# Token tiles handed one by one across four post-norm stage ends, with the post-norm's scale vectors brought by DMA

## The chip, the core and the metric

The kernel runs on one core of a Trainium2 chip. The metric is the device time of one execution in microseconds (us): 3312.12 us, the median of 3 runs (3311.99 to 3313.26). Everything is float32.

## The reference, cut to what matters

The input is 256 tokens of 2048 features, so two *token tiles* of 128 tokens. Two layers run one behind the other, and then a third block of another kind. A layer is

```python
for layer in range(2):
    h = rmsnorm(x, pre_mix_g[layer])
    mix = even_mixer(h, ...) if layer == 0 else rglru_mixer(h, ...)   # ends in ... @ w_out
    x = x + rmsnorm(mix, post_mix_g[layer])                           # stage end
    f = sq_relu_mlp(rmsnorm(x, pre_mlp_g[layer]), mlp_w1[layer], mlp_w2[layer])
    x = x + rmsnorm(f, post_mlp_g[layer])                             # stage end

def rmsnorm(x, g):
    y = x * lax.rsqrt(jnp.mean(x * x, axis=-1, keepdims=True) + EPS)
    return y * g
```

So there are four *stage ends with a post-norm*: the output of a stage (2048 features a token) is normed over all its features, scaled by a vector g of 2048 numbers, and added to the residual stream x. The new x is normed again, which is the input of the next stage's first product. End 1 follows the attention's output product, end 2 the first MLP, end 3 the recurrent mixer's output product, end 4 the second MLP. The third block ends with a final norm and its own scale vector.

## The kernel before, in words

**Products.** A weight matrix is read in *units*: two blocks of 128 rows by 512 columns, 512 KB. SyncE issues the DMA of each unit into a ring of 8 slots (`raw`). ScalarE rounds a unit to `hi` (`conv`, line 597), VectorE writes `lo = raw - hi` (line 1071); both have a ring of 4. TensorE then does three matmuls of 512 columns for each block and token tile: x_hi hi, x_lo hi, x_hi lo (`unit`, lines 1736 to 1738). A unit is thus 12 matmuls, 6 a token tile. The activations stand as the stationary operand, features on the partitions, in `xt_h`/`xt_l` and `ht_h`/`ht_l`.

**Chunks.** A *chunk* is 512 output columns, normally 8 units, summed in the PSUM pair `pair[0]`, one bank a token tile. Every engine runs the same program `model`, chunk after chunk, and each engine does its part strictly in the order in which it is written; semaphores tie the engines together. In a chunk TensorE takes the first two and the last two units token tile by token tile and the others for both, so that a chunk's first token tile can be read out while the second is still being summed. ScalarE and VectorE convert units three ahead of the chunk that they read out (`AHEAD`). The four chunks of a stage's last product go to `acc` (VectorE, `evac`: copied for "set", added for "add"), and ScalarE squares what was written (line 651) with the sums per token.

**An MLP** has four groups; each group is four "relu2" chunks and four "add" chunks. Layer 0 runs group 0 and then a hardware loop of three turns; layer 1 runs group 0, a loop of two turns, and group 3 with steps for the third block among it. GpSimd sets `acc` to zero ahead of each MLP, so that all groups can add.

**A stage end** is the first chunk of the next stage, which has a `lead` of kind "post". TensorE first spreads the scale vector: four `gain` matmuls (line 1868, two instructions each) put 512 columns of g on all partitions in the two banks `misc_ps`. VectorE waits until both token tiles of the last chunk are read out and squared, sums the squares, ScalarE takes the root (line 743), VectorE the reciprocal (`norm_factor`). Then for each 512 columns n (`residual`): acc times factor times g for two token tiles (line 1277, two instructions), x += acc for both at once (line 1281). TensorE transposes that part of x (`turn_part`, line 1894, eight transposes of 128 by 128) into `turn_ps` or `pair[1]`, ScalarE writes its `hi` with the next norm's scale (`part`, line 758, four instructions of 256 elements) and then squares x (line 770), VectorE writes the `lo` (`lo_part`, line 1298, four of 256). Parts 0 and 1 are turned ahead of the first weight matmul, part 2 behind units 0 and 1, part 3 behind units 2 and 3. Of the stage's units three are converted before the stage end begins.

**The final norm** gets its vector in the same way: a matmul behind each of the last four chunks (`spread_final_gain`, line 2159).

Of the kernel before, what the change touches and what calls it, by code (L numbers as in the profile page):

```python
# [34 lines left out]
P = 128  # L35
SEQ = 256
M = SEQ // P
D = 2048
# [20 lines left out]
G_POST_MIX, G_POST_MLP, G_FINAL, G_ROWS = 0, 8, 16, 20  # L59
# [35 lines left out]
    "squared": "scalar: sums of squares of a chunk are written, tmp is free",  # L95
# [3 lines left out]
    "gain_ready": "tensor: a chunk of a gain is spread over the partitions",  # L99
    "x_ready": "vector: a chunk of the residual stream is up to date",  # L100
    "acc_zero": "gpsimd: acc is zero for an MLP's sums",
    "gained": "vector: a chunk of x times the final gain is in acc",
# [88 lines left out]
N_LOADS, N_PARAM_LOADS = 15, 12  # L191
# [5 lines left out]
Lead = namedtuple("Lead", "kind gain_row gain_col parts x_hi x_lo")  # L197
# [35 lines left out]
def build(nc, i, out):  # L233
# [15 lines left out]
    with ExitStack() as ctx:  # L249
# [18 lines left out]
        grows = at("grows", 170, [CH])  # L268
# [104 lines left out]
        class Program:  # L373
# [26 lines left out]

            HALF = {"psum_free_act": "half_free_act", "psum_free_dve": "half_free_dve"}
# [6 lines left out]
        class Sync(Program):  # L408
            def setup(self):
# [21 lines left out]
                for dst, src in (  # L431
                    (grows[0:8], i["post_mix_g"].rearrange("l (c n) -> (l c) n", n=CH)),
                    (grows[8:16], i["post_mlp_g"].rearrange("l (c n) -> (l c) n", n=CH)),
                    (grows[16:20], i["final_g_2"].rearrange("(c n) -> c n", n=CH)),
# [22 lines left out]
            def chunk(self, kind, w, units=8, width=CH, lead=None, slot=None, prep=None, **_):  # L457
                src, t0, col0 = w
                if lead and lead.kind == "post":
                    self.T.add("x_ready", 4)  # L460
# [108 lines left out]
        class Scalar(Program):  # L569
# [112 lines left out]
            def chunk(self, kind, w, units=8, width=CH, prev=None, lead=None, to=None, dst=None, n=0, ss=True,  # L682
                      more=False, final=False, gate=None, lru=None, constant=False, slot=None, slot1=None, prep=None, bank=0,
                      **_):
                T, ps = self.T, pair[bank]
                T.add("pe", units)
                if lead:
                    self.lead(lead)
                    self.evac(kind, ps, 0, dst, width)
                    self.conv()  # L690
                else:
                    at = self.turn_slot(prev, units)
                    for j in range(units):
# [3 lines left out]
                        if prep is not None:  # L697
                            self.prepare(prep, j)
                        if slot is not None:
# [3 lines left out]
                        if j == 1 and self.unsquared is not None:  # L703
# [14 lines left out]
                        if j == 6 and lru is not None:  # L718
                            self.lru_root(lru)
                self.evac(kind, ps, 1, dst, width)  # L720
                if kind in self.TURNED:
# [6 lines left out]

            def lead(self, lead):

                kind = lead.kind
                if kind == "post":
                    self.root(D)
# [1793 lines left out]
```

## Time and profile before

| | |
|---|---|
| median of 3 runs | 3312.12 us |
| the profiled execution | 3304.36 us |
| its span in the trace | 3302.6 us |
| mean granted clock of TensorE | 0.986 |
| busy: TensorE, weight load, VectorE, ScalarE, GpSimd | 3213.3, 2638.0, 1892.6, 1594.0, 255.4 us |
| DMA | 595.37 MB, mean 180 GB/s |

The trace is one profiled execution. Busy time is the time in which an engine has an instruction under way; matmuls overlap (one of 512 columns lasts 0.39 us in the trace, though the next starts sooner), so TensorE's distance from start to start says more than its busy time. The granted clock is the share of full speed that TensorE was given. The chain of waits is followed back from the last instruction to what released it, and so names what the end depended on.

### The profile page before, as it was taken

How to read it: one execution, taken by the hardware profiler on the slowest of the kernel's cores; microseconds unless marked ns; L12 is line 12 of the kernel's file. 1: busy time of each engine (PE TensorE's matmuls, PEld its weight loads, DVE VectorE, ACT ScalarE, POOL GpSimd, SP SyncE). 2: the span in 40 equal slices, each digit the busy share in tenths (PEclk: the TensorE clock that was granted, in tenths of full speed). 3: DMA queues.
4: the chain of work that ended last, by engine and by line, in shares of the span. 5: the costliest groups of instructions: out<-in, count | busy, mean ns of one | idle time of the engine just before them, and what ended most of it. 6: DMA issues, size and time to landing. Idle time of an engine off the chain costs nothing.

```text
span 3302.6 us, 39931 instructions
## 1 busy us (share of the span) xinstructions
PE 3213.3 (97%) x15159; PEld 2638.0 (80%) x15159; DVE 1892.6 (57%) x2142; ACT 1594.0 (48%) x2197; POOL 255.4 (8%) x331
## 2 busy tenths in 40 slices
PE   8999999999999999999999999999989999999998
PEld 6777788888888787778888888878778888888886
DVE  4667654555555667555554555558876545455445
ACT  5655544444444568554444445543354543444443
POOL 0000000000000020010830005610000000000000
PEclk9999999999999999989999999989999999999999
DMA  6544556556565455555656557756545665665663
GB/s 225 147 147 141 153 184 196 187 186 191 191 186 188 146 176 164 181 153 189 193 183 196 187 186 229 237 179 194 160 131 169 187 189 191 191 191 191 192 191 115
DMA packets 321365, 595.37 MB, mean 180 GB/s; under 512 B 32740, under 2 KB 39828, under 8 KB 320936
## 3 DMA queue, kind: packets, MB, share of 16 engines
q1 hardware_dynamic: 321192, 592.98, 57.5%
q8 instruction: 119, 1.95, 0.2%
q14 instruction: 54, 0.44, 0.0%
HBM read 581.89 MB, written 11.01 MB: 180 GB/s over the span
## 4 chain that ended last, share of the span: by engine, by line
PE 90%; DVE 6%; ACT 3%; issue 1%; SPq 0%; DMA 0%; ACTq 0%; DVEq 0%
PE pair L1736 28%; PE pair L1738 28%; PE pair L1737 28%; DVE lo L1071 2%; PE turn_ps L1767 1%; ACT hi L597 1%; PE pair L2055 1%; PE pair L1949 0%; PE misc_ps L1868 0%; PE pair L2056 0%; DVE conv_o L1176 0%; PE turn_ps L1894 0%; PE pair L1894 0%; PE misc_ps L1964 0%; DVE lru_h L1352 0%
## 5 line engine op out<-in xcount | busy, mean ns | idle before, releaser
L1071 DVE TENSOR_TENSOR lo<-raw,hi 128x1024 fp32r<-128x1024 f32 x1084 | 1341.4, 1241 | 1261.8 <-ACT hi L597 1251.2
L597 ACT ACTIVATE hi<-raw 128x1024 fp32r<-128x1024 f32 x1084 | 1144.1, 1059 | 1399.2 <-PE pair L1738 1377.0
L1736 PE MATMUL pair<-hi,xt_h 128*128 128x512 f32 (+1 forms) x2784 | 1100.7, 395 | 19.2 <-DVE lo L1071 7.1
L1738 PE MATMUL pair<-lo,xt_h 128*128 128x512 f32 (+1 forms) x2784 | 1086.2, 390 | 0.0
L1737 PE MATMUL pair<-hi,xt_l 128*128 128x512 f32 (+1 forms) x2784 | 1085.1, 390 | 0.0
L1736 PEld LDWEIGHTS pair<-hi,xt_h 128*128 128x128 f32 x2784 | 526.2, 189 | 142.0 <-issue 15.7
L1738 PEld LDWEIGHTS pair<-lo,xt_h 128*128 128x128 f32 x2784 | 525.5, 189 | 110.7
L1737 PEld LDWEIGHTS pair<-hi,xt_l 128*128 128x128 f32 x2784 | 526.5, 189 | 104.1
L1736 PE MATMUL pair<-hi,ht_h 128*128 128x512 f32 x1504 | 587.6, 391 | 4.9 <-DVE ht_l L1185 3.6
L1738 PE MATMUL pair<-lo,ht_h 128*128 128x512 f32 x1504 | 585.3, 389 | 0.0
L1737 PE MATMUL pair<-hi,ht_l 128*128 128x512 f32 x1504 | 585.2, 389 | 0.0
L1736 PEld LDWEIGHTS pair<-hi,ht_h 128*128 128x128 f32 x1504 | 282.3, 188 | 66.7 <-DVE ht_l L1185 4.0
L1738 PEld LDWEIGHTS pair<-lo,ht_h 128*128 128x128 f32 x1504 | 282.3, 188 | 58.8
L1737 PEld LDWEIGHTS pair<-hi,ht_l 128*128 128x128 f32 x1504 | 282.4, 188 | 57.8
L624 ACT ACTIVATE stg<-pair,stat 128x512 f32<-128x512 f32 x126 | 86.7, 688 | 114.1 <-PE pair L1738 112.9
L2292 POOL MEMSET acc<- 128x4096 f32 x3 | 10.6, 3521 | 920.1 <-DVE xres L1281 547.2
L1111 DVE TENSOR_TENSOR acc<-pair,acc 128x512 f32<-128x512 f32 x96 | 66.0, 687 | 24.1 <-PE pair L1738 24.1
L2165 POOL TENSOR_TENSOR lru_h<-ht_h,ht_l 128x1024 f32<-128x1024 f32 x4 | 9.6, 2402 | 865.9 <-ACT gate_i L801 865.9
L1767 PE MATMUL turn_ps<-ident,stg 128*128 128x128 f32 x508 | 65.9, 272 | 0.0
L1767 PEld LDWEIGHTS turn_ps<-ident,stg 128*128 128x128 f32 x508 | 58.9, 140 | 6.8
L651 ACT ACTIVATE tmp<-acc 128x512 f32<-128x512 f32 x80 | 49.3, 617 | 19.1 <-DVE acc L1111 17.2
L1161 DVE TENSOR_TENSOR ht_l<-turn_ps,ht_h 128x1024 fp32r<-128x1024 f32 x43 | 52.4, 1219 | 4.2 <-ACT ht_h L672 4.2
(269 smaller groups left out, 1669.1 us busy)
## 6 DMA issues: line engine op xcount, KB each, us to landing
raw<-in_mlp_w SPq DMA_DIRECT2D x512, 512.0 KB, 4.1
raw<-in_w_gate SPq DMA_DIRECT2D x88, 512.0 KB, 4.2
raw<-in_w_up SPq DMA_DIRECT2D x88, 512.0 KB, 4.2
raw<-in_w_down SPq DMA_DIRECT2D x88, 512.0 KB, 4.1
raw<-in_even_w_in SPq DMA_DIRECT2D x68, 512.0 KB, 3.7
raw<-in_odd_w_in SPq DMA_DIRECT2D x64, 512.0 KB, 3.9
raw<-in_w_in SPq DMA_DIRECT2D x64, 512.0 KB, 3.9
raw<-in_even_w_out SPq DMA_DIRECT2D x32, 512.0 KB, 3.6
```

Of the source, the lines that this page charges most:

```text
L597: nc.scalar.activation(hi[:, r], raw[:, slot], ACT.Copy).then_inc(sems["hi_ready"], 1)
L624: a = nc.scalar.activation(to, ps[:, m, 0:width], func, scale=st(RS + m))
L651: a = nc.scalar.activation(tmp[:, m], src[:, m, n * CH:(n + 1) * CH], ACT.Square, accum_out=st(sums + 4 * m + n))
L1071: nc.vector.tensor_tensor(lo[:, r], raw[:, slot], hi[:, r].bitcast(F32), ALU.subtract).then_inc(sems["lo_ready"], 1)
L1111: a = nc.vector.tensor_tensor(dst[:, m], ps[:, m], dst[:, m], ALU.add)
L1161: a = nc.vector.tensor_tensor(to[1], turn_ps[:], to[0].bitcast(F32), ALU.subtract)
L1736: nc.tensor.matmul(to, xh[:, t0 + k, tok], h[:, k], start=s, stop=False)
L1737: nc.tensor.matmul(to, xl[:, t0 + k, tok], h[:, k], start=False, stop=False)
L1738: mm = nc.tensor.matmul(to, xh[:, t0 + k, tok], l[:, k], start=False, stop=e)
L1767: a = nc.tensor.transpose(turn_ps[:, k, m * P:(m + 1) * P], stg[:, m, k * P:(k + 1) * P], ident[:])
L2055: nc.tensor.matmul(to, b_w[:, j, 2 + ri], u2[:, g, 0:HALF], start=True, stop=False)
L2292: nc.gpsimd.memset(acc[:], 0.0).then_inc(sems["acc_zero"], 1)
```

## The change

- **Tiles.** At the four ends the work on x is cut in eight tiles of 512 features by 128 tokens, in the order `TILES` = (part, token tile) (0,0) (1,0) (0,1) (1,1) (2,0) (2,1) (3,0) (3,1).
- **Tail.** The last chunk of each of these stages (`tail`) takes its last *four* units token tile by token tile (before: two; in the chunk of 4 units at end 1 all four). TensorE turns tile 0 ahead of the last unit's second token tile, and tile 1 behind the chunk. ScalarE and VectorE don't convert ahead across the end: the first three units of the next stage are converted inside `post_lead`. ScalarE does a root of a constant at the end of the tail.
- **Lead.** Each token tile has its own squares, root and reciprocal. `residual` is one instruction a tile. A tile has 4 transposes, 4 ScalarE and 4 VectorE instructions of 128 elements. TensorE takes the first four units for token tile 0 and then for token tile 1, with the turns of tiles 2 to 7 in between.
- **Scale vectors.** ScalarE issues one DMA per 512 numbers, from DRAM to all 128 partitions (256 KB written), into one buffer `gain`; VectorE multiplies `acc` by it in place one chunk later (`apply_gain`), the last chunk's in the lead (`tile_gain`). A load waits until the one before is used. The final norm's vector comes in the same way. All matmuls that spread vectors go, and three DMAs of the setup.
- **Around it.** The first group of each MLP writes `acc` ("set"), GpSimd's zeroing goes; squares are taken only in the group that ends a stage; layer 0's loop has two turns and its last group stands by itself. In the tail of end 4 ScalarE's step `prepare(.., 6)` moves up to unit 4, ahead of the load of the scale vector.

```diff
@@ Scalar.chunk
-                    for j in range(units):
+                    for j in range(units - AHEAD if tail else units):
...
+                        if j == (4 if units == 8 else 0 if tail else 1) and stage is not None:
+                            name, l = STAGES[stage]
+                            self.load_gain(4 * stage + n, i[name][l, n * CH:(n + 1) * CH])
+                        if j == 3 and final:
+                            self.load_gain(16 + n, i["final_g_2"][n * CH:(n + 1) * CH])
...
+                if tail:
+                    nc.scalar.activation(unused, eps_col, ACT.Sqrt)
+                    return
+            def load_gain(self, q, src):
+                if q:
+                    self.eng.wait_ge(sems["gain_used"], q)
+                nc.scalar.dma_start(gain[:], src.partition_broadcast(P)).then_inc(sems["gain_loaded"], 16)
+            def post_lead(self, lead): 
+                self.out_square(0)
+                self.tile_root(0)
+                self.convs(2)
+                self.tile_hi(lead, 0, 0)
+                self.conv()
+                self.tile_hi(lead, 1, 0)
+                self.out_square(1)
+                self.tile_root(1)
+                self.conv()
+                self.tile_hi(lead, 0, 1)
+                self.tile_hi(lead, 1, 1)
+                for p, m in TILES[0:4]:
+                    self.x_square(p, m)
+                self.conv()
+                self.tile_hi(lead, 2, 0)
+                self.tile_hi(lead, 2, 1)
+                self.conv()
+                self.tile_hi(lead, 3, 0)
+                self.tile_hi(lead, 3, 1)
+                self.conv()
+                self.x_square(2, 0)
+                self.x_square(2, 1)
+                self.conv()
+                self.x_square(3, 0)
+                self.x_square(3, 1)
+                self.convs(2)
+                self.root(D)
@@ Vector
+                        if j == (0 if units == 4 else 3) and stage is not None and n:
+                            self.apply_gain(n - 1)
+            def post_lead(self, lead): 
+                self.sum_squares(0)
+                self.tile_gain(0)
+                self.tile_factor(0)
+                self.residual(0, 0)
+                self.residual(1, 0)
+                self.conv()
+                self.tile_lo(lead, 0, 0)
+                self.conv()
+                self.evac(*self.unread)
+                self.tile_lo(lead, 1, 0)
+                self.sum_squares(1)
+                self.conv()
+                self.tile_factor(1)
+                self.residual(0, 1)
+                self.conv()
+                self.residual(1, 1)
+                self.tile_lo(lead, 0, 1)
+                self.tile_lo(lead, 1, 1)
+                self.residual(2, 0)
+                self.residual(2, 1)
+                self.conv()
+                self.tile_lo(lead, 2, 0)
+                self.tile_lo(lead, 2, 1)
+                self.tile_gain(1)
+                self.residual(3, 0)
+                self.conv()
+                self.residual(3, 1)
+                self.tile_lo(lead, 3, 0)
+                self.tile_lo(lead, 3, 1)
+                self.convs(4)
+                self.norm_factor(SSX, RS, "rs_ready")
-                for m in range(M):
-                    ins = nc.vector.scalar_tensor_tensor(acc[:, m, cols], acc[:, m, cols], st(RPOST + m),
-                                                         misc_ps[:, n % 2], ALU.mult, ALU.mult)
-                ins = nc.vector.tensor_tensor(xres[:, :, cols], xres[:, :, cols], acc[:, :, cols], ALU.add)
+                nc.vector.scalar_tensor_tensor(xres[:, m, cols], acc[:, m, cols], st(RPOST + m), xres[:, m, cols],
+                                               ALU.mult, ALU.add).then_inc(sems["x_ready"], 1)
@@ Tensor.chunk
+                head = 4 if post or units == 4 and tail else 2
+                end = 4 if tail else 2
+                            if post:
+                                self.tile_wait(lead, j, 1 if whole else m)
+                                if (m, j) in ((0, 3), (1, 0), (1, 2), (1, 3)):
+                                    self.turn_tile(2 + ((0, 3), (1, 0), (1, 2), (1, 3)).index((m, j)))
+                            if tail and (m, j) == (1, units - 1):
+                                self.turn_tile(0)
...
+                            if post and whole:
+                                self.turn_tile(2 + j)
...
+                if tail:
+                    self.turn_tile(1)
-            def spread_final_gain(self, n):
```

## Rows read from the trace of the kernel before

**Rows 1.** The page's chain that ended last, by engine.
```profile
PE 90%; DVE 6%; ACT 3%; issue 1%; SPq 0%; DMA 0%; ACTq 0%; DVEq 0%
```

**Rows 2.** TensorE's timeline, last group: start us, us, engine, line, operation, out<-in [idle before <-releaser].
```profile
3235.98 0.39 PE L1738 MATMUL pair<-lo,ht_h 128*128 128x512 f32 x1
...
3236.66 0.39 PE L1738 MATMUL pair<-lo,ht_h 128*128 128x512 f32 x1
...
3238.03 0.50 PE L1736 MATMUL pair<-hi,ht_h 128*128 128x512 f32 x1
```

**Rows 3.** Groups by line: count | busy us, mean ns of one | idle before.
```profile
L1071 DVE TENSOR_TENSOR lo<-raw,hi 128x1024 fp32r<-128x1024 f32 x1084 | 1341.4, 1241 | 1261.8 <-ACT hi L597 1251.2
...
L597 ACT ACTIVATE hi<-raw 128x1024 fp32r<-128x1024 f32 x1084 | 1144.1, 1059 | 1399.2 <-PE pair L1738 1377.0 <-PE pair L2144 11.8 <-PE misc_ps L1917 5.7
...
L880 ACT ACTIVATE o_diff<-misc_ps 128x128 f32<-128x128 f32 x16 | 4.3, 269 | 0.0
...
L1435 DVE SCALAR_TENSOR_TENSOR probs<-scores,stat,probs 128x128 f32<-128x128 f32 x8 | 2.8, 352 | 0.3
```

**Rows 4.** TensorE's timeline, end 1.
```profile
359.96 0.39 PE L1738 MATMUL pair<-lo,xt_h 128*128 128x512 f32 x1
...
366.85 1.97 PE L1894 MATMUL turn_ps<-ident,xres 128*128 128x128 f32 x8 [4.60 <-DVE xres L1281]
...
374.65 0.80 PE L1736 MATMUL pair<-hi,xt_h 128*128 128x512 f32 x1
...
379.06 0.40 PE L1737 MATMUL pair<-hi,xt_l 128*128 128x512 f32 x1
...
382.26 1.03 PE L1894 MATMUL turn_ps<-ident,xres 128*128 128x128 f32 x8
383.05 0.48 PE L1736 MATMUL pair<-hi,xt_h 128*128 128x512 f32 x1
```

**Rows 5.** Timelines: the lead chunk's second read-out at end 1; end 4.
```profile
400.60 0.69 ACT L624 ACTIVATE stg<-pair,stat 128x512 f32<-128x512 f32 x1 [0.24 <-PE pair L1738]
...
2160.19 0.39 PE L1738 MATMUL pair<-lo,ht_h 128*128 128x512 f32 x1
...
2202.39 0.69 ACT L624 ACTIVATE stg<-pair,stat 128x512 f32<-128x512 f32 x1 [0.24 <-PE pair L1738]
```

**Rows 6.** Table loads of ScalarE ahead of line 743's root, groups by line.
```profile
L743 ACT ACT_TABLE_LOAD x5 | 6.4, 1283 | 0.1
```

**Rows 7.** Windows, end 1: stretch, busy by engine, then granted TensorE clock, DMA share, GB/s.
```profile
366.00:372.00 6.00, 5.15 (x16) 3.32 (x17) 5.61 (x10) 2.79 (x8) 0.00 (x0) 0.50 0.00 0
```

**Rows 8.** VectorE's and ScalarE's timelines, end 1.
```profile
361.32 0.68 DVE L1111 TENSOR_TENSOR acc<-pair,acc 128x512 f32<-128x512 f32 x1
362.04 0.63 ACT L651 ACTIVATE tmp<-acc 128x512 f32<-128x512 f32 x1 [1.89 <-DVE acc L1111]
...
363.40 0.16 DVE L1260 TENSOR_REDUCE stat<-stat 128x2 f32<-128x8 f32 x1 [1.40 <-ACT tmp L651]
363.60 0.29 ACT L743 ACTIVATE stat<-stat 128x2 f32<-128x2 f32 x1 [0.23 <-DVE stat L1260]
...
364.13 1.41 DVE L1277 SCALAR_TENSOR_TENSOR acc<-acc,stat,misc_ps 128x512 f32<-128x512 f32 x2
...
368.86 1.57 ACT L758 ACTIVATE xt_h<-turn_ps,col 128x256 fp32r<-128x256 f32 x4 [4.96 <-PE turn_ps L1894]
369.73 1.66 DVE L1298 SCALAR_TENSOR_TENSOR xt_l<-turn_ps,col,xt_h 128x256 fp32r<-128x256 f32 x4 [0.36 <-ACT xt_h L758]
```

**Rows 9.** DMA issues: out<-in, queue, count, KB each, median us to landing.
```profile
b_raw<-in_b_re SPq DMA_DIRECT2D x1, 256.0 KB, 4.1
b_raw<-in_b_im SPq DMA_DIRECT2D x1, 256.0 KB, 6.1
```

**Rows 10.** TensorE's timeline behind two other gaps of the kernel.
```profile
1350.13 0.50 PE L1736 MATMUL pair<-hi,ht_h 128*128 128x512 f32 x1 [3.60 <-DVE ht_l L1185]
...
2331.93 0.79 PE L2067 MATMUL misc_ps<-u,c_w 128*128 128x128 f32 x2 [3.13 <-DVE h_im L1584]
```

More of the change, by code:

```diff
@@ L94 @@
     "split_done": "vector: their lo part too, the turned PSUM is free",
-    "squared": "scalar: sums of squares of a chunk are written, tmp is free",
+    "squared": "scalar: sums of squares of a chunk, or of a token tile of it, are written, tmp is free",
     "tot_ready": "vector: the tokens' sums of squares are added up",
@@ L98 @@
     "rs_ready": "vector: its reciprocal, the stage's rms factors",
[L99 to L102, printed above, removed]
+    "gain_loaded": "a chunk of a gain is on all partitions (16 a chunk)",
+    "gain_used": "vector: it is multiplied in",
+    "x_ready": "vector: a chunk of the residual stream (of a token tile, in a lead with a norm) is up to date",
     "out_ready_dve": "vector: the first half of the features of a token tile is normed",
@@ L698, in chunk @@
                             self.prepare(prep, j)
+                            if tail and j == 4:
+                                self.prepare(prep, 6)
                         if slot is not None:
@@ L1188, in chunk @@
             def chunk(self, kind, w, units=8, width=CH, prev=None, lead=None, to=None, dst=None, n=0, ss=True,
-                      more=False, final=False, gate=None, lru=None, constant=False, slot=None, slot1=None, bank=0, **_):
+                      more=False, final=False, gate=None, lru=None, constant=False, slot=None, slot1=None, bank=0,
+                      stage=None, tail=False, **_):
                 T, ps = self.T, pair[bank]
@@ L1199, in chunk @@
                     at = self.turn_slot(prev, units)
-                    for j in range(units):
+                    for j in range(units - AHEAD if tail else units):
                         if j == units - 1:
@@ L1781, in chunk @@
                     self.eng.wait_ge(sems["k0_copied"], 8)
-                if lead:
+                post = lead is not None and lead.kind == "post"
+                if lead and not post:
                     self.lead_first(lead)
                 at = self.turn_slot(prev, units)
-                for j in range(0, units, 2):
-                    first, last = j == 0, j == units - 2
-                    for half in range(2):
-                        if j + half == at:
-                            self.turn(prev)
-                        if last and half == 0 and prev and kind in ("add", "set"):
-                            self.eng.wait_ge(sems["split_done"], T.at("split_done"))
-                        self.lead_wait(lead, j + half)
-                        self.part_wait(ready, j + half, 0)
-                        self.unit(x, ps, self.tile(x_tiles, width, j + half), first and half == 0, last and half == 1,
-                                  width, (0,) if first or last else (0, 1))
-                        if not (first or last):
-                            self.prepare(prep, j + half)
+                head = 4 if post or units == 4 and tail else 2
@@ L1798, in chunk @@
                             if slot is not None:
[L1799 removed]
+                                self.mix_at(slot + j)
                             if slot1 is not None:
[L1801 to L1815 removed]
@@ L2365, in ht_part, with mlp_group @@
             return ht_h[:, 4 * j:4 * j + 4], ht_l[:, 4 * j:4 * j + 4]
[L2367 removed]
+        def mlp_group(e, w1, w2, g, lead=None, params=False, prep=False, stage=None):
             prev = None
@@ L2375, in mlp_group @@
             for n in range(NCH):
-                e.chunk("add", (w2, g * KT, n * CH), x=HT, dst=acc_cols(n), n=n, prev=prev if n == 0 else None,
-                        more=n < NCH - 1, prep=4 + n if prep else None)
+                e.chunk("set" if lead else "add", (w2, g * KT, n * CH), x=HT, dst=acc_cols(n), n=n,
+                        prev=prev if n == 0 else None, ss=stage is not None, more=n < NCH - 1, stage=stage,
+                        tail=stage is not None and n == NCH - 1, prep=4 + n if prep else None)
                 if params and n == 1:
@@ L2399, in swiglu_group @@
             for n in range(NCH):
-                e.chunk("add", (w_down2, g * KT, n * CH), x=HT, dst=acc_cols(n), n=n, units=2 * hidden, ss=False,
+                e.chunk("set" if lead else "add", (w_down2, g * KT, n * CH), x=HT, dst=acc_cols(n), n=n, units=2 * hidden, ss=False,
                         prev=prev if n == 0 else None, more=n < NCH - 1, final=last)
```

301 lines of the change are left out of this document (181 added, 120 removed).

## The prediction

> **What bounds the kernel now.** The page's chain first: TensorE carries 90% of what the end depended on, VectorE 6%, ScalarE 3% [rows 1]. A stream of weight matmuls at full clock starts one every 0.227 us (three in 0.68 us) [rows 2], so 2.72 us a unit, 21.76 us a chunk. ScalarE needs 1.06 us and VectorE 1.24 us to convert a unit [rows 3], under half of that. So only what makes TensorE stop or run slower counts, and TensorE's timeline shows where: at the stage ends. At end 1 the last weight matmul starts at 359.96, its successor would be due at 360.19, the first of the next chunk starts at 374.65 [rows 4], and the chunk is over at 400.43 (its second read-out starts at 400.60, 0.17 behind) [rows 5]. That is 40.24 us for 21.76 us of matmuls: **18.5 us lost**. End 4, by the same three readings, loses 2202.22 - 2160.42 - 21.76 = 20.0 us [rows 5]; ends 2 and 3, by the rows of the same pattern (of which the first and the last of four stand), 18.1 and 19.4. **Sum 76.0 us.** Ends 3 and 4 hold a table load of 1.28 us that ends 1 and 2 don't [rows 6].
>
> In a loss stand: a chain over read-out, squares, root, two factors and the residual until the first transpose at 366.85, 4.60 us after TensorE had nothing left [rows 4]; then transposes at half speed, eight in 1.97 us against about 0.8 us at full speed at 382.26 [rows 4], since the granted clock is 0.50, the lower level of 1.2 GHz [rows 7]; then ten weight matmuls in 4.41 us (374.65 to 379.06), 2.1 us more than they need [rows 4].
>
> **The change at one end, step by step.** I walk the three in-order queues with these prices. Token tile of a unit on TensorE 6 x 0.227 = 1.36 us; four transposes 0.45 (half of 382.26 to 383.05, and the slower start behind them) [rows 4]. Convert: 1.06 then 1.23, the next start 0.97 and 1.15 later [rows 3]. Read-out 0.68; square of a token tile 0.73 with its sum (362.04, and the reduce starts at 363.40 after two); reduce 0.16; root 0.29; one residual instruction 0.70 (two of its shape in 1.41) [rows 8]. The 128-element instructions don't stand in a trace with these operands. Upper bound: the 256-element ones, four in 1.57 and 1.66, so 0.39 and 0.41 each [rows 8]. Lower: half, 0.20. The step from 512 elements (0.70) to 256 (0.41) takes off 0.15 per 128 on VectorE, so 0.27; ScalarE 0.28, for which 128 elements out of PSUM at 0.269 speak [rows 3] (VectorE's nearest lasts 0.352, of which its successor waits less). I take 0.27 and 0.28: a tile is about 1.1 us on each.
>
> A rule of the Trainium skill weighs against small tiles here. In "VectorE: DVE Perf Modes", section "The TRN2 errata", it says that every instruction pays a fixed latency, and to use 512 elements or more. By its figures (120 cycles and the elements at 0.96 GHz) an instruction of 128 is an estimate of 0.26 us, so the sum is the same by either; halving the instruction doesn't halve its price, and that is in it.
>
> Zero is the end of the tail's token tile 0. Read-out to 0.86, square to 1.63, reduce, root to 2.16; VectorE's scale multiply meanwhile; reciprocal, residual of tile 0 at 2.57 to 3.31, of tile 1 to 3.97. TensorE needs the first at 4.08, after three units of token tile 1: **no wait for tile 0**, and none for tile 1. The tail ends at 6.34, with its two turns in it. Units 0 and 1 of the next stage need their conversion: ScalarE 2.12 to 4.14, VectorE at 3.90 and, behind tile 0's lo, at 6.35. TensorE starts at 6.34, unit 1 at 7.70.
> - Unit 2 stands in VectorE's queue behind read-out 1, tile 1's lo and the second reduce, and is ready at 10.49. TensorE waited from 9.06: **1.46**. Unit 3: **0.20**.
> - Token tile 1 of units 0 to 3 runs with turns 3 to 5 in between until 20.7. Unit 4 needs tile (2,1)'s first half, which is behind four squares and a conversion on ScalarE and a conversion and tile 4 on VectorE: ready 21.9. **1.25**.
> - Units 4 and 5, turns 6 and 7, until 28.28. Unit 6 is queued behind tile 7: hi to 29.53, convert 30.50, lo of the unit 31.77. **3.52**, the longest. Unit 7 stands behind two squares: **0.84**.
> - The next chunk waits for the read-out, which waits for the norm factor: **0.63**.
>
> Waits 7.9 us, eight turns 3.6 us: **11.5 us lost per end, 46.0 for four.** With 0.41 and 0.39 a small instruction the same walk gives 14.7 us, with 0.20 it gives 9.9.
>
> **The scale vectors.** The loads of an end's last vector go out just before it is wanted (1.77 in the walk, and TensorE has 0.77 of slack at tile 0). At ends 2 and 3 ScalarE issues it behind the tail's unit 7, near -4; at end 4 only behind the moved `prepare` copies, near -1.4; at end 1 behind the multiply of vector 2, near -1.6. 256 KB loads land 4.1 and 6.1 us after issue [rows 9]; a broadcast of one row stands nowhere, so these are my bounds. At 4.1 nothing waits at ends 1 to 3, at 6.1 ends 1 and 4 wait 2 us. I take 0.5 each: **1.0**. If the vectors are late, what is queued behind the multiply is VectorE's reciprocal and both residuals, and TensorE at turn 0. The other 15 loads have half a chunk or more, and sit in ScalarE's idle time; a load waits for the multiply before it, behind it ScalarE's conversions, which have three units of lead.
>
> **The clock.** TensorE comes into the end at full clock and no longer stands still for 4.6 us. Of its new gaps only the 3.52 (and a turn before it) is near those after which rows show the lower level: a gap of 3.60 left matmuls at full speed (0.50 us), one of 3.13 was followed by slow ones (0.79) [rows 10]. Even chances; a fall costs up to the 2.1 us of above, less the 0.84 and part of the 0.63 that it covers. I take 0.8 an end: **3.2**. The Trainium skill, "TensorE: Matmul & The Clock Gate", section "Why this matters for your kernels", warns that an idle gap between bursts of matmuls throws the clock back. Taken to hold at every end it would make this term 6.4, so 3 us more.
>
> **The rest.** Of the final norm's four matmuls three stand between chunks: 3236.66 to 3238.03 plus a slow second matmul, less 0.23, is 1.24 us each [rows 2]: **-3.7**; the fourth stands beside the last read-out. Layer 0's loop loses a turn: between nothing and 0.6, I take **-0.5**. The root of a constant takes the 1.28 us table load out of the chain of ends 3 and 4 (it lies in ScalarE's wait for the tail; without that cover it would cost its 1.28); this is already in the walk. VectorE's scale multiplies move into chunks where it is idle for half the time, GpSimd's zeroing and 48 chunk squares were on no path: nothing. Costs nothing as well: a "set" instead of an "add".
>
> **Sum.** 76.0 - 46.0 - 1.0 - 3.2 + 3.7 + 0.5 = **30 us less**. The profiled execution took 3304.36 us (span 3302.6), so 3274 by it. It ran 7.8 us under the median of the runs; I take the same difference off the median: 3312.1 - 30 = **3282 us**.
>
> **The rivals.**
> - *Small instructions cost like large ones.* VectorE and ScalarE lengthen the waits to 14.7 an end, the ends cost 12.7 more: 3295. For it: the fixed part is most of an instruction already. Against: 0.269 for 128 elements out of PSUM. 15%.
> - *The gaps shrink.* Small instructions at 0.20 and no fall of the clock: 9.9 an end, 9.6 less: 3272. 10%.
> - *The vectors come late at all four ends.* The landing decides: from about 6 us on ends 1 and 4 wait, from 7 us all four. At 10 us each end waits some 5 more and the clock falls: about 25 us, 3307, no change that counts. For it: a DRAM row read 128 times on a queue that nothing used before. 6%.
> - *Slower: the clock stays low through the lead.* Its place is the stretch from the wait for unit 2 to that for unit 6. If each of the gaps of 1.46, 1.25 and 3.52 us drops the clock, products take 2.72 us a token tile and turns twice as long; all of a lead at half speed adds 21.8 + 3.6 less the 7.9 of waits that it covers, 17.5 an end, 70 in all: 3350. It decides from 8.3 us an end, nearly half of the lead at half speed. For it: a 3.13 us gap did it [rows 10]. Against: the 3.60 us one didn't, and two of the three here are under half of that. 7%.
> - *The waits don't move as written*, for instance a conversion stays behind and the end is as long as before, less the gain matmuls: 3306. 4%.
>
> **How the numbers follow.** My forecast has 58% with a range of its own of 3275 to 3292. The cases with 15% and 10% are faster too. Time from no change can be told at about 0.2%, 6.6 us, so faster is under 3305.5: 58 + 15 + 10 and half of the late vectors and unmoved waits, 0.88. Within: 0.05. Slower: 0.07. The range leaves out the slow clock and half of the two cases near no change above, and half of the shrunk gaps below: 3270 to 3303.
>
> **What would show it.** In the trace after: tile 0's transposes start within 0.5 us of a matmul, with no idle before; TensorE's gaps at an end are four or five, the longest near 3.5 us just ahead of unit 6, released by VectorE's conversion; from the tail's last product to the lead's second read-out about 32.5 us where it was 40.4; a tile's four small instructions take 1.1 to 1.2 us; the granted clock is 1.00 in each end but for at most one dip; line 2159's matmuls are gone. It is wrong if turn 0 waits for a scale vector, if the clock is 0.5 for more than a unit or two, or if the lead is as long as before.

## The result

| | us, median (runs) | ratio to the kernel before, 95% interval |
|---|---|---|
| kernel before | 3312.47 (4) | 1 |
| changed kernel | 3280.05 (4; 3277.36 to 3282.88) | 0.9902 [0.9885, 0.9919] |
| changed kernel, repeated later (after_again) | 3282.89 (4), before 3308.99 (15) | 0.9915 [0.9900, 0.9930] |

The change is worth 26 to 32 us; 3282 (3270 to 3303) was predicted. That the first median lies within 2 us of the forecast is partly luck: the four executions of the changed kernel spread over 5.5 us, and the repeat gives 6 us less of a gain than the first comparison. The profiled execution of the changed kernel took 3277.36 us, its span is 3274.8, which is 27.8 under the span of before. The page's chain that ended last, by engine, where [rows 1] stood:
```profile
PE 88%; DVE 7%; ACT 4%; issue 1%; DMA 0%; SPq 0%; ACTq 0%
```
and the windows of the four ends (stretch, busy by engine, granted clock, DMA share, GB/s), where [rows 7] showed 0.50:
```profile
358.00:400.00 42.00, 34.90 (x162) 26.73 (x161) 29.88 (x61) 28.59 (x69) 0.00 (x0) 1.00 0.44 138
1082.00:1124.00 42.00, 35.03 (x165) 27.51 (x164) 30.24 (x61) 29.09 (x69) 0.00 (x0) 1.00 0.42 133
1405.00:1447.00 42.00, 36.17 (x165) 28.59 (x164) 30.47 (x62) 29.28 (x69) 0.00 (x0) 0.96 0.40 113
2138.00:2180.00 42.00, 36.03 (x163) 28.14 (x162) 30.64 (x61) 29.12 (x69) 8.26 (x10) 0.96 0.49 153
```
TensorE is busy for 35 to 36 of 42 us, and the clock dips briefly at ends 3 and 4 alone.

TensorE's gaps at end 2 of the changed kernel, from its timeline (start us, us, engine, line, operation, out<-in [idle before <-releaser]):
```profile
1086.21 0.39 PE L1901 MATMUL pair<-lo,ht_h 128*128 128x512 f32 x1
1086.44 0.60 PE L2018 MATMUL turn_ps<-ident,xres 128*128 128x128 f32 x4
1086.80 0.48 PE L1899 MATMUL pair<-hi,ht_h 128*128 128x512 f32 x1
...
1092.76 0.47 PE L1899 MATMUL pair<-hi,xt_h 128*128 128x512 f32 x1 [1.12 <-DVE lo L1164]
...
1104.60 0.50 PE L1899 MATMUL pair<-hi,xt_h 128*128 128x512 f32 x1 [1.42 <-DVE xt_l L1420]
...
1114.58 0.47 PE L1899 MATMUL pair<-hi,xt_h 128*128 128x512 f32 x1 [3.31 <-DVE lo L1164]
...
1116.95 0.47 PE L1899 MATMUL pair<-hi,xt_h 128*128 128x512 f32 x1 [0.74 <-DVE lo L1164]
...
1121.69 0.50 PE L1899 MATMUL pair<-hi,xt_h 128*128 128x512 f32 x1 [0.38 <-ACT stg L631]
```
These answer to [rows 4]: where TensorE stood for 4.60 us and then turned at half speed, the first transposes follow a matmul after 0.23 us, and what is left is five short stops, ahead of unit 2, unit 4, unit 6, unit 7 and the next chunk. The three longer stops (1.1 to 1.2, 1.4 and 3.3 us) stand at all four ends, the two short ones (0.74 and 0.38) only at ends 1 and 2, where the clock did not fall. Here are ScalarE and VectorE ahead of the longest stop:
```profile
1111.09 1.14 ACT L831 ACTIVATE xt_h<-pair,col 128x128 fp32r<-128x128 f32 x4 [2.07 <-PE pair L2018]
1112.11 1.07 ACT L604 ACTIVATE hi<-raw 128x1024 fp32r<-128x1024 f32 x1
1113.05 0.64 ACT L813 ACTIVATE tmp<-xres 128x512 f32<-128x512 f32 x1
```
```profile
1111.75 1.13 DVE L1420 SCALAR_TENSOR_TENSOR xt_l<-pair,col,xt_h 128x128 fp32r<-128x128 f32 x4 [2.08 <-ACT xt_h L831]
1113.21 1.23 DVE L1164 TENSOR_TENSOR lo<-raw,hi 128x1024 fp32r<-128x1024 f32 x1 [0.33 <-ACT hi L604]
```
Unit 6's conversion (line 604, then 1164) is queued behind the last token tile, and TensorE starts 0.14 us after VectorE is through. A tile's four small instructions take 1.11 to 1.16 us on either engine.

At end 1 the last vector is late (VectorE's timeline):
```profile
358.31 0.69 DVE L1202 TENSOR_TENSOR acc<-pair,acc 128x512 f32<-128x512 f32 x1 [1.19 <-PE pair L1901]
...
360.75 0.69 DVE L1407 TENSOR_TENSOR acc<-acc,gain 128x512 f32<-128x512 f32 x1 [0.80 <-DMA gain<-in_post_mix_g]
361.36 0.15 DVE L1390 RECIPROCAL stat<-stat 128x1 f32<-128x1 f32 x1
```
ScalarE issued that load at 357.15, and VectorE had it 3.6 us later, after an idle time of 0.80 us. Turn 0 starts at 362.36, that is 0.17 us after its place in the stream of matmuls, and in the repeat TensorE idles 0.44 us ahead of it. By the DMA view, the loads of one row to all partitions took:
```profile
gain<-in_post_mix_g ACTq DMA_DIRECT2D x8, 256.0 KB, 4.2
gain<-in_post_mlp_g ACTq DMA_DIRECT2D x8, 256.0 KB, 4.2
gain<-in_final_g ACTq DMA_DIRECT2D x4, 256.0 KB, 3.2
```

**Where the 27.8 us are.** The loss of an end after is counted as before, to the lead's second read-out: the time from the read-out of the tail's first token tile, less 27.2 us of matmuls (5.44 of the tail, 21.76 of the chunk).

| part | before | after | difference |
|---|---|---|---|
| four ends | 18.5 + 18.1 + 19.4 + 20.0 = 76.0 | 13.5 + 12.7 + 12.7 + 13.1 = 52.0 | -24.0 |
| final norm, from end 4 to VectorE's last read-out | 1087.47 | 1083.64 | -3.8 |
| gaps on TensorE in layer 0's loop | 0.74 + 0.55 | none | -1.3 |
| a fall of the clock in the stage ahead of end 3 | 0.60, 0.54 in two 4 us windows | 0.75, 0.82 | -1.7 |
| two falls of the clock in the attention stage that before's trace lacks | | | +3.4 |
| rest | | | -0.4 |

The two rows on falls of the clock, and part of the loop's, lie between executions and not between kernels. The two falls in the attention stage stand in every trace of this study but before's, that of before_loop_two (the old kernel there) among them; and the repeat of the changed kernel has a gap of 0.89 us at the loop, and a span of 3280.9. No run separates the tiles from the way in which the vectors come; the 24 us belong to both together.

### The profile page after: what moved, and what is told of

The parts are those of the page before. It is cut to its first block, busy times and chain, and to the rows that moved or that the text cites. A ratio compares the mean times of both kernels' runs of the same rounds, so it can differ in the third digit from the quotient of the medians.

```text
span 3274.8 us, 39528 instructions
## 1 busy us (share of the span) xinstructions
PE 3179.9 (97%) x15119; PEld 2621.4 (80%) x15119; DVE 1903.4 (58%) x2218; ACT 1579.9 (48%) x2173; POOL 247.5 (8%) x328
## 4 chain that ended last, share of the span: by engine, by line
PE 88%; DVE 7%; ACT 4%; issue 1%; DMA 0%; SPq 0%; ACTq 0%
PE pair L1899 28%; PE pair L1901 27%; PE pair L1900 27%; DVE lo L1164 2%; ACT hi L604 1%; PE turn_ps L1930 1%; PE pair L2228 1%; PE pair L2122 1%; PE pair L2229 0%; DVE xt_l L1420 0%; DVE conv_o L1267 0%; ACT tmp L813 0%; PE misc_ps L2137 0%; DVE lru_h L1516 0%; ACT xt_h L831 0%
## 5 line engine op out<-in xcount | busy, mean ns | idle before, releaser
L1202 DVE TENSOR_TENSOR acc<-pair,acc 128x512 f32<-128x512 f32 x72 | 49.5, 687 | 26.0 <-PE pair L1901 26.0
L679 ACT ACTIVATE ht_h<-turn_ps 128x1024 fp32r<-128x1024 f32 x43 | 43.5, 1012 | 0.1
L1179 DVE TENSOR_TENSOR stg<-stg 128x1024 f32<-128x1024 f32 x32 | 39.1, 1222 | 0.0
```

Of the source, the lines that this page charges most:

```text
L679: nc.scalar.activation(to[0], turn_ps[:], ACT.Copy).then_inc(sems["split_hi"], 1)
L1179: nc.vector.tensor_tensor(stg[:], stg[:], stg[:], ALU.mult).then_inc(sems["staged"], 1)
L1202: a = nc.vector.tensor_tensor(dst[:, m], ps[:, m], dst[:, m], ALU.add)
```

## The experiments

All but the last are the changed kernel with one edit (order_loads has two). "End" is the time from the read-out of the tail's first token tile to the lead's second read-out, in each run's trace.

| run | us (runs) | ratio to before | ends 1 to 4, us |
|---|---|---|---|
| after_again | 3282.89 (4) | 0.9915 [0.9900, 0.9930] | 41.1, 39.9, 39.9, 41.8 |
| conv_first | 3279.30 (4) | 0.9910 [0.9895, 0.9926] | 39.4, 38.2, 40.2, 38.6 |
| squares | 3273.99 (4) | 0.9890 [0.9871, 0.9909] | 40.1, 37.6, 38.5, 38.0 |
| order | 3261.09 (5) | 0.9852 [0.9838, 0.9865] | 32.4, 32.3, **42.4**, 33.1 |
| loads_only | 3281.27 (4) | 0.9912 [0.9896, 0.9929] | 41.0, 39.9, 39.9, 40.2 |
| order_loads | **3249.03** (5) | **0.9817** [0.9803, 0.9830] | 32.3, 32.4, 32.4, 33.1 |
| tail_two | 3289.55 (4) | 0.9937 [0.9921, 0.9952] | + 2.7 at 2 to 4: 44.1, 42.5, 42.5 |
| no_root | 3281.87 (4) | 0.9915 [0.9900, 0.9931] | 41.2, 40.0, 40.9, 41.8 |
| before_loop_two | 3310.34 (10) | 1.0003 [0.9994, 1.0012] | |

(The kernel before took 3307.8 to 3309.0 beside these. In tail_two the first token tile's read-out comes 2.7 us later at three ends, which is added.)

**conv_first.** The conversions go ahead of the last tiles:
```
 Scalar:  tile_hi(lead, 2, 1)            Vector:  residual(3, 1)
-conv(); tile_hi 3,0; tile_hi 3,1; conv() -tile_lo 3,0; tile_lo 3,1; convs(4)
-x_square 2,0; 2,1; conv()
+convs(3); tile_hi 3,0; tile_hi 3,1      +conv(); tile_lo 3,0; conv(); tile_lo 3,1; convs(2)
+x_square 2,0; 2,1
```


> The changed kernel, with the conversions of units 6 and 7 of the lead moved ahead of tile (3, 1)'s two copies on ScalarE, and on VectorE ahead of tile (3, 0)'s and tile (3, 1)'s lo parts. Theory (my forecast's): the 3.3 us gap ahead of unit 6 and the 0.75 us behind it are the order of the conversions alone. Both then go, but the norm factor of the next chunk hangs on the same chain of squares and residuals; a walk of the three queues with the trace's durations gives a loss per end of 11.5 us where it gives 13.45 now, with a new wait of about 3.9 us ahead of units 8 and 9's second read or the read-out: 4 x 1.9 = 8 us faster, about 3272. Rival A: the gap is all there is, and nothing waits later: 4 x 4.1 = 16 us faster, about 3264. Rival B: the tiles become late instead, ahead of units 6 and 7, by as much as the conversions went ahead: within 2 us of 3280. The clock at the ends: if it falls by the idle time of 3.3 us, it falls in neither unit 6's place at any end.

Both gaps went, and 3.26 us stood ahead of the next chunk instead (5.2 at end 3). TensorE's timeline at end 2:
```profile
1122.93 0.50 PE L1901 MATMUL pair<-hi,xt_h 128*128 128x512 f32 x1 [3.26 <-ACT stg L631]
...
1124.22 0.52 PE L1903 MATMUL pair<-lo,xt_h 128*128 128x512 f32 x1
1124.54 0.63 PE L1901 MATMUL pair<-hi,xt_h 128*128 128x512 f32 x1
```
The end is 1.7 us shorter there (1.9 expected), and by the next chunk's first read-out nothing is left: 60.30 us from the same start, 60.35 in the changed kernel. At ends 1 and 3 that read-out even comes 0.8 to 1.7 us later than in the changed kernel and its repeat. The matmuls of 0.63 us behind the wait are the clock: it fell in or around the new wait at all four ends, and no stop stands right behind it that could take the fall in. So the gap that was filled came back as a wait in the next chunk, and what remained went to the clock. At end 3 there is a third part: ScalarE idles 1.50 and 0.42 us ahead of two conversions there, for weights that SyncE issued late (see order). Rival A has fallen, and so has the 8 us: the medians differ by 3.6 us in favour of the edit, and the runs overlap. The time is the one that rival B named, but not by its cause: nothing waits ahead of units 6 and 7.

**squares.** ScalarE's eight squares of x alone:
```
-tile_hi 0,1; tile_hi 1,1; x_square x4; conv(); tile_hi 2,0; 2,1; conv(); 3,0; 3,1; conv(); x_square x2; conv(); x_square x2; convs(2)
+x_square(0, 0) ahead of tile_root(1); x_square(1, 0) behind its conv(); (0, 1) behind tile_hi 1,1; (1, 1) behind a conv()
+tile_hi 2,0; 2,1; conv(); x_square 2,0; 2,1; tile_hi 3,0; 3,1; convs(4); x_square 3,0; 3,1
```


> The changed kernel with the squares of x alone moved on ScalarE (each up to one or two tiles ahead; those of (2, 0) and (2, 1) ahead of the last two tiles, those of (3, 0) and (3, 1) behind the conversions of units 6 to 9); the conversions of units 6 and 7 stay behind the last tile, VectorE's order is untouched. conv_first moved those conversions alone and gained nothing (3279.3 against 3282.9 for the changed kernel, with a wait of 3.3 us in the next chunk). Theory: the two gaps have different causes, the 1.4 us ahead of unit 4 the squares, the 3.3 us ahead of unit 6 the conversions; the walk gives 9.4 us per end where the changed kernel has 13.45: 4 x 4 = 16 us faster than it, about 3267, with the gap ahead of unit 6 at about 3.6 us and no wait at unit 4 over 0.2 us. Rival: as with the conversions, what is won ahead of unit 4 is waited for later (ahead of unit 6, over 4.5 us): under 4 us faster.

At end 2 these are the gaps left in TensorE's timeline:
```profile
1093.68 0.47 PE L1899 MATMUL pair<-hi,xt_h 128*128 128x512 f32 x1 [1.12 <-DVE lo L1164]
1113.84 0.77 PE L1899 MATMUL pair<-hi,xt_h 128*128 128x512 f32 x1 [3.31 <-DVE lo L1164]
```
The gap ahead of unit 4 is gone, the 3.31 us one is the same to the hundredth: two causes, as the theory has it. The size is half of what was expected: 8.9 us by the medians, 2.3 by end 2 (39.94 to 37.64, where the walk had 36.6). At end 2 the clock falls behind the 3.31 us gap (0.77 us for the matmul above), and the stops that took such a fall in have gone. At end 3 the clock did not fall, and a wait for weights stands in its place, on ScalarE and then on TensorE:
```profile
1438.34 1.06 ACT L604 ACTIVATE hi<-raw 128x1024 fp32r<-128x1024 f32 x1 [2.52 <-DMA raw<-in_mlp_w]
```
```profile
1443.60 0.50 PE L1899 MATMUL pair<-hi,xt_h 128*128 128x512 f32 x1 [1.62 <-ACT stg L631]
```
That these two make up the whole difference is not shown.

**order and order_loads.** The same instructions on both engines in another order, found with the walk of the three queues (and one semaphore wait of VectorE more, ahead of the residual of (3, 0)):
```
Scalar: out_square 0, root 0, convs 3, hi(0,0), hi(1,0), out_square 1, x_square, root 1, conv, x_square x2,
        hi(0,1), hi(1,1), x_square, conv, hi(2,0), hi(2,1), conv, x_square, convs 2, hi(3,0), conv,
        x_square, hi(3,1), conv, x_square x2
Vector: sum 0, factor 0, residual(0,0), (1,0), convs 2, lo(0,0), evac, conv, sum 1, lo(1,0), factor 1,
        residual(0,1), conv, residual(1,1), lo(0,1), residual(2,0), (2,1), gain 0, lo(1,1), gain 1, conv,
        lo(2,0), lo(2,1), residual(3,0), convs 3, residual(3,1), lo(3,0), conv, lo(3,1), conv
```


> The changed kernel with the same instructions on ScalarE and VectorE in the four leads, in another order: three conversions ahead of the first tile's copies, the eight squares of x spread between the tiles as soon as their residuals are there, the conversions of units 4 to 7 early, VectorE's multiplication by the last gain vector late (behind the residual of (2, 1)), where the DMA has landed. Theory: what the ends still lose (about 12 us each) is for more than half the order of work on two engines that are not full; the walk gives 5.2 to 5.6 us per end with no wait over 0.7 us, so 4 x 8 = 32 us faster, about 3248, and the clock stays at its upper level through all four ends (half a us to 1 us each at the two that fell). Rival: the chain of squares, root, reciprocal to the next chunk's read-out sets the end whatever the order: a wait of 3 to 4 us in the next chunk, 8 us faster at most, about 3272.

Three ends came out at 32.3 to 33.1 us, that is 5.1 to 5.9 lost (5.2 to 5.6 expected); one wait is longer than the 0.7 us that were expected as the most, 1.10 us at end 4. The third end took 42.4. TensorE's, ScalarE's and SyncE's timelines of order there:
```profile
1430.51 0.80 PE L1902 MATMUL pair<-hi,xt_h 128*128 128x512 f32 x1 [7.44 <-DVE xt_l L1421]
```
```profile
1427.62 1.06 ACT L604 ACTIVATE hi<-raw 128x1024 fp32r<-128x1024 f32 x1 [9.55 <-DMA raw<-in_mlp_w]
```
```profile
1378.33 12.61 SPq L461 DMA_DIRECT2D raw<-in_mlp_w  x6
1419.07 0.37 SPq L487 DMA_DIRECT2D b_raw<-in_b_re  x1
1419.48 2.27 SPq L487 DMA_DIRECT2D b_raw<-in_b_im  x1
1421.80 14.94 SPq L461 DMA_DIRECT2D raw<-in_mlp_w  x11
```
TensorE names VectorE's tile; VectorE had waited for ScalarE, and ScalarE for weights that left only at 1421.80, behind two loads that wait for the last residual. The waits by releaser, SyncE's queue, give the price: 
```profile
SPq L487 <- DVE xres L1448: 28.1, 1, 28.1
```
The changed kernel has the same wait (28.2 us); loads_only below shows that it costs nothing there, where those weights are wanted later. Hence:
```
-                if params and j == 0:
+                if params and j == (1 if isinstance(e, Sync) else 0):
                     e.s5_params(0)
```


> The reordered leads of the run called order, and one thing more: the queue of SyncE issues the two loads of the state space parameter B (which wait for the last residual of the third stage end) behind the weight loads of that group's second chunk, and not behind those of its first. In order's trace TensorE stood 7.4 us ahead of unit 4 of the lead at the third end, with ScalarE 9.6 us ahead of a conversion for its weights, which SyncE held behind those two loads; the other three ends took 32.4, 32.3 and 33.1 us from the first token tile's read-out to the second read-out of the lead, the third 42.4. Theory: the queue of SyncE alone makes the difference; the third end takes 32.5 to 33, and the kernel is 9.5 us faster than order, a ratio to the kernel before of about .9825 (3251 where before is 3308.5). Rival: the weights are late by the DMA engines themselves, which were busy at that place in the changed kernel as well: under 3 us faster than order.

The third end fell from 42.4 to 32.4 us, of which 7.4 is the wait and the rest the clock that it had thrown back (0.50 from 1428 to 1436 in order's windows). The time fell by 12.1 us; the 2 us beyond the end are of the size by which executions differ. The rival, that the DMA engines themselves are late, has fallen. The windows of order_loads at the four ends (stretch, busy by engine, granted clock, DMA share, GB/s):
```profile
358.00:390.00 32.00, 31.31 (x152) 25.44 (x151) 28.19 (x60) 27.53 (x68) 0.00 (x0) 1.00 0.53 171
1074.00:1106.00 32.00, 31.33 (x152) 25.45 (x151) 28.42 (x60) 27.29 (x67) 0.00 (x0) 1.00 0.52 164
1393.00:1425.00 32.00, 31.33 (x153) 25.40 (x152) 28.58 (x60) 27.10 (x67) 0.00 (x0) 1.00 0.52 144
2119.00:2152.00 33.00, 31.57 (x153) 25.66 (x153) 29.40 (x60) 27.39 (x67) 8.55 (x10) 1.00 0.61 191
```
VectorE is now busy for 88 to 89% of these stretches: by this and TensorE's 31.3 of 32 us little is left to win by order alone.

**loads_only.** The edit to SyncE's queue in the changed kernel.


> The changed kernel with SyncE's two loads of B behind the weight loads of the group's second chunk, and nothing else: the part of order_loads that is not the leads' order. In the changed kernel's trace SyncE waits 28.2 us there for the last residual. Theory: the weights that it holds back are not wanted before that in this order, the third end stays at 39.9 us: no change, within 2 us of 3282.9. Rival: they cost the changed kernel as well, 3 us or more faster.

3281.27 against 3282.89, the third end 39.94 in both: no change, as the theory says. In the changed kernel's order the loads cost nothing; in conv_first and squares, which draw work forward too, ScalarE did wait for weights at end 3 (see there), so each reorder was measured together with this cost.

**tail_two.**
```
-                end = 4 if tail else 2
+                end = 4 if tail and units == 4 else 2
```


> The changed kernel, with the closing group of the stage's last chunk back to two units at the three ends of eight units (ends 2 to 4). Forecast's theory: the first token tile's product ends 4.1 us ahead of the last matmul and not 6.8, less 1.36 us of it being the second product's own time: the chain read-out, square, sum, root, reciprocal, residual, worth about 4 us, is then uncovered; the walk gives a wait of 2.0 us ahead of the first turn and 2.3 us more per end, 3 ends: 7 us slower, about 3287. Rival: the gaps later in the lead (1.4 and 3.3 us) hang on the same chain and take no more time than before, so that a late start is not made up: same 7; or they absorb it because their releasers are not set by the start: 0 to 2 us slower.

```profile
1088.85 0.66 PE L2018 MATMUL turn_ps<-ident,xres 128*128 128x128 f32 x4 [1.83 <-DVE xres L1445]
```
6.7 us slower by the medians, with a wait of 1.83 us ahead of the first turn at all three ends, and each gap behind it about as long as before: the late start is not made up. Ends 3 and 4 are 2.6 and 2.3 us longer than in the changed kernel (2.3 expected); the 4.2 of end 2 hold a longer fall of the clock. The four-unit tail carries about 7 us of the change at these three ends.

**no_root.**
```
-                    nc.scalar.activation(unused, eps_col, ACT.Sqrt)
```


> The changed kernel without the dummy square root behind the last read-out of a stage, which calls the activation table of the root ahead of time. Theory: the table load (1.28 us in the trace) then stands between the square and the root in the chain to the first turn where the table in ScalarE was another one; it is covered at ends 1 and 2 if the table there is already the root's, else not: 0.7 us per end by the walk, 1.3 to 2.8 us slower in all, 3281 to 3283. Rival: nothing, since the chain has 1 us of air ahead of the first turn; within 0.5 us.

Inconclusive in time (1.0 us under the repeat, the runs overlap). The trace shows the cost all the same. At ends 3 and 4 ScalarE's timeline has the table load in the chain, right behind the square; at end 3:
```profile
1410.99 1.28 ACT L818 ACT_TABLE_LOAD   x1
```
The first turn comes 4.09 and 4.19 us behind the read-out at ends 3 and 4, against 3.88 with the early root: the air ahead of turn 0 takes in most of the 1.28 us. But ScalarE's conversions queue behind the load, so that the stop ahead of unit 2 comes 0.8 and 1.0 us later, and this is not made up: end 3 takes 40.9 us where it took 39.9 in the three traces with the same lead and the early root. So the walk's 0.7 us an end stands in the trace (end 4 is blurred by a longer fall of the clock), and the rival that the air hides it all has fallen; two such ends are too little for the medians.

**after_again** and **before_loop_two.**


> The changed kernel once more, as the measure for the runs of this study. Its ratio to the kernel before was 0.990; the same is expected here, 0.989 to 0.992. Its trace is read for where the clock falls: in the first trace it fell in the 3.3 us gap at the third and the fourth end and not at the first two; if that is chance, it falls at another choice of ends here, if it hangs on the place, at the same two.

The clock fell at all four ends, where it fell at two in the first trace: the place does not decide. The window of this run behind the 3.31 us gap of end 2, where the first trace has 1.00:
```profile
1114.00:1118.00 4.00, 2.51 (x6) 1.99 (x7) 2.45 (x2) 3.82 (x11) 0.00 (x0) 0.68 0.36 111
```
The edit of the other one is `loop(2)` and a written-out last group in layer 0:


> The kernel before, with the first layer's MLP as the changed kernel has it: its last group of four written out behind a loop of two turns instead of in a loop of three. Forecast's theory: a turn's end costs TensorE what its gap shows, so one turn fewer gives 0.5 us. The two traces say more: the kernel before had two gaps on TensorE between the first and the second end (0.74 and 0.55 us), the changed one none of 0.1 us or more, so 1.3 us; by the medians neither can be told from no change, and the trace's stretch between the two ends decides. Rival: the gaps come from the squares written in every group, which only the changed kernel leaves out in its inner groups: then both gaps stay, 0 us.

No change in time can be told. The kernel before has two gaps on TensorE between ends 1 and 2, from its timeline,
```profile
734.98 0.49 PE L1736 MATMUL pair<-hi,xt_h 128*128 128x512 f32 x1 [0.74 <-issue]
...
913.53 0.49 PE L1736 MATMUL pair<-hi,xt_h 128*128 128x512 f32 x1 [0.55 <-issue]
```
and before_loop_two has one:
```profile
737.03 0.49 PE L1736 MATMUL pair<-hi,xt_h 128*128 128x512 f32 x1 [0.29 <-issue]
```
All ten traces with a loop of two turns lack the second gap, so it goes with the turn, as forecast. The first is in this run, which still writes the squares in every group, shorter than in the repeat of the changed kernel, which doesn't (0.29 and 0.89 us): the squares are out as its cause. Over all eleven traces it is between under 0.1 us (five of them) and 0.89, so the 1.3 us of the first comparison is half chance.

## Why the prediction was right, step by step

- **Tile 0 and tile 1 wait for nothing.** Right at ends 2 to 4. At end 2 the first residual is done 0.8 us ahead of its turn (0.77 in the walk). At end 1 the late vector uses the air up, and turn 0 is 0.2 us late (0.2 to 0.5 us of idle time ahead of it in the other traces with this multiplication in front). That is one of the prediction's own signs of being wrong, met at one end of four and at a price that its term for the vectors holds. That the four-unit tail is what spares TensorE the wait, tail_two shows: 1.83 us of wait without it, 2.0 by the walk.
- **Six waits, 7.9 us.** Right in place: 1.12, 0, 1.42, 3.31, 0.74 and 0.38 idle at end 2 where 1.46, 0.20, 1.25, 3.52, 0.84 and 0.63 stood. The idle times add up to 7.0 us. Counted from when TensorE's next start was due they are 7.8, since it loses about 0.16 us more in each than the idle time shows (1.28 us between a due start and the start behind the idle of 1.12), and behind each the following start is late by 0.1 more. (The walk's own times give 1.43 for the first and 3.49 for the longest, 0.03 less than it puts down.)
- **Eight turns at 0.45.** 0.36 us to the next matmul (1086.44 to 1086.80), and that one holds its successor up by 0.08: 0.44.
- **Together 11.5 us an end.** 12.1 at the undisturbed end 2, from the first tile's last product to the start of the next chunk at 1121.69; by the second read-out, which stands behind a conversion on ScalarE, 12.7. That is why the stretch from the tail's last product to this read-out is 34.2 us and not 32.5. So the four ends came out 6.0 us above the 46.0 of the walk (52.0), where the prediction had set 4.2 aside for vectors and clock. 2.4 of it is a step of the reckoning and no loss of TensorE's: the loss of before was read at ScalarE's read-out, the walk of after at TensorE's next start, and only in the new kernel does the read-out lag behind that start (0.6 us an end more). Another 2.4 are the waits and turns, 12.1 us an end for 11.5; 0.8 is the late vector of end 1.
- **Small instructions at 0.27 and 0.28.** Right: a tile takes 1.11 to 1.16 us, its successor starts 1.02 to 1.04 later. The rivals at 0.40 and 0.20 are out.
- **The vectors, 1.0.** About right: 0.8 us at end 1 (40.68 against 39.93 us; VectorE idles 0.80 for the load), no wait for the load at end 4, where ScalarE issued the load 2.9 us ahead of the first tile's read-out (2135.31), not 1.4.
- **The clock, 3.2.** A size that a single trace can't fix. The 3.31 us gap stands in six traces (the first, the repeat, squares, loads_only, tail_two, no_root), four times each, and the clock fell in or behind 20 of the 24. A fall often costs nothing by the second read-out (39.94 us with it, 39.93 without, at end 2), since the waits of 0.74 and 0.38 take it in. The dearest case that compares like with like is the repeat's end 4, where a longer fall costs 1.5 (41.8 against 40.25 with a short one). The forecast's even chances were too kind, and its price too high: 0.8 an end at even chances is 1.6 a fall, more than its own bound of 2.1 less the 0.84 covered. The product is near by luck (the repeat's ends are 2 us longer than the first trace's). The reading of [rows 10] that stood behind the even chances, a gap of 3.60 us that left the clock up, was chance too: see the last section. The slow rival, a clock that stays low from the 1.46 gap on, has fallen: no gap under 1.9 us at an end moved it.
- **Final norm -3.7, loop -0.5.** -3.8; and for the loop 0.55 us of idle time in one trace, too little for the medians of before_loop_two to show.
- **The sum.** 28 us by the spans and 26 to 32 by the medians, for 30. The ends gave 24.0 us of the 25.8 forecast with vectors and clock; before's trace, which lacks two falls of the clock that all others have, takes off 3.4 more, and its longer fall ahead of end 3 gives 1.7 back.

What the forecast did not see: it took the waits for the price of small tiles, while more than half of each end's 12 us was queue order on two engines with room. Alone, the squares paid 2.3 us an end and the conversions nothing by the next chunk; together, with the early conversions of units 2 and 3, the new order paid 7.6. The likely reason is that the conversions that go forward need the places that the squares leave, and the read-out of the next chunk needs the squares early; this, and the share of the late multiplication by the last vector, is argued and not taken apart by a run.

## What to carry to other kernels

Write down the in-order queues of all engines around a stall, with durations from the trace: the walk hit six waits to within 0.34 us each, and the same walk turned into a search found, with the two loads of SyncE moved, the 34 us that a hand-made order had left. Test each reorder past the place where it acts: a gap filled can come back as a wait in the next chunk, and work drawn forward can run into a DMA queue that stands behind an unrelated wait, which costs nothing until then. Where a wait sits beside a clock fall, compare several traces, since the fall is a matter of chance between executions.

## What the hardware showed that was not expected

- The granted clock fell in or behind 20 of 24 gaps of 3.31 us. Elsewhere in the kernel stands a gap of 3.60 us, once in each of the eleven traces ([rows 10], 1350.13): in those of before and after the clock stayed up there, in the other nine it fell in or behind it. TensorE's timeline in the repeat of the changed kernel, where the matmul lasts 0.80 us and not 0.50:
```profile
1342.03 0.80 PE L1899 MATMUL pair<-hi,ht_h 128*128 128x512 f32 x1 [3.60 <-DVE ht_l L1276]
```
So one trace can't say whether a gap of this length costs clock; which executions it hits is open here.
- Behind a group of four transposes in a stream of weight matmuls the next matmul keeps its successor waiting 0.31 us where others take 0.227; behind a stop likewise.
- One row of 2 KB spread over 128 partitions by ScalarE's DMA queue landed after 3.2 to 4.2 us in the median (3.0 to 6.5 in all), in the median no slower than the 256 KB loads of [rows 9] (4.1 and 6.1); the issue held ScalarE's queue for 0.34 us.
